# State-space mixer: the order of GpSimd's products and sums, and the depth of two buffers

## The chip, the cores and the metric

One core of a Trainium2 chip runs the whole program. The time is the device time of one launch in microseconds (us). Three runs of the kernel before gave 2972.24, 2974.73 and 2974.77 us, with a median of 2974.73 us.

## The reference

Three layers on one sequence of 256 tokens of width 2048, in fp32: differential attention and an MLP; a state-space (S5) mixer with a gated projection (GLU) and an MLP; a hybrid layer of forgetting attention and a delta-rule recurrence. The change touches only the S5 mixer, whose core is this:

```python
def s5_mixer(h, a_re, a_im, log_dt, b_re, b_im, c_re, c_im, d_skip, w_glu):
    ...
    u = h.astype(F32).reshape(B, S, S5_GROUPS, S5_GROUP)      # 128 groups of 16 channels, state 64

    def per_sequence(u_s):
        bu_re = jnp.einsum('sgc,gpc->sgp', u_s, bb_re)
        bu_im = jnp.einsum('sgc,gpc->sgp', u_s, bb_im)
        _, _, x_re, x_im = lax.associative_scan(
            _scan_combine, (a_seq_re, a_seq_im, bu_re, bu_im), axis=0)
        return jnp.einsum('sgp,gcp->sgc', x_re, cr) - jnp.einsum('sgp,gcp->sgc', x_im, ci)

    y = lax.map(per_sequence, u).reshape(B, S, D)
    y = y + d_skip.astype(F32) * h.astype(F32)
    g = jax.nn.gelu(y).astype(h.dtype)
    val, gate = jnp.split(g @ w_glu, 2, axis=-1)
    return val * jax.nn.sigmoid(gate)
```

The complex recurrence x[s] = a x[s-1] + bu[s] is solved by turning it: the inputs are multiplied by the phases of a (a cosine and a sine table), a real scan with the magnitude of a runs over the turned values, and the scanned states are turned back with the same tables.

## The kernel before, in words

Nearly all of the program is a stream of fp32 matrix products on TensorE. Weights are loaded from HBM in units, split by ScalarE (`wH`, L1785) and VectorE (`wL`, L2498) into a high and a low part, and multiplied (L987, L988, L994). Between the first MLP and the GLU product lies the S5 stage. It takes the 128 groups in 16 blocks, numbered 0 to 15, of 8 groups; the 256 tokens are folded by 4 (`S5_L`), so that a scan runs over 64 positions (`S5_N`).

The order is written out by hand. Each engine has its own loop over k = 0 to 20, and `s5_steps()` (from L204) lists the same order once more to number the semaphore values. The steps of a block b, with the names used below:

- **p(b)**, ScalarE, L2135: the tokens of the block, scaled, into `up`. **u(b)**, TensorE, L1282: four transposes into one PSUM bank. **t(b)**, ScalarE, L2143: that bank copied into `ut`, "the turned inputs". t(b) waits for u(b) and, from b = 4, for y(b-4), which read the place that is overwritten.
- **d(b)**, ScalarE, L2151: the decay table `dd` of the block.
- **g(b)**, TensorE, L1296: the products of `ut` with the input matrices `gt` into the bank `wk[b % 2]`; it waits for t(b) and for the scan z(b-2), which read that bank.
- **rotate and combine**, VectorE, L3014 and L3022: the phases applied, into `rc[b % 3]` and the bank.
- **z(b)**, VectorE, L3031: two scans, into `rc`. **n(b)**, ScalarE, L2158: a negated copy of one half.
- **zc(b)**, GpSimd, L899: the scanned states times the cosine table; it waits for z(b). **zs(b)**, L901: times the sine table; it waits for n(b). **x(b)**, L905: the sum of the two, into `xs[b % 2]`; it waits for its own zs(b) and, from b = 2, for y(b-2).
- **y(b)**, TensorE, L1311 to L1313: 24 products, of `ut`, of `xs` and of the output matrices; it waits for x(b). **e(b)**, ScalarE, L2171: two GELUs of the result.
- once in two blocks, for the pair j: **h(j)**, TensorE, L1326: eight transposes, after e(2j+1); **H(j)**, ScalarE, L2189: the high part `hH`; **hL(j)**, VectorE, L3046: the low part.

What stands in a row in step k of the loop: on TensorE u(k), g(k-1), y(k-4), and with k even and at least 6 also h((k-6)/2), in steps 16 to 19 then a unit of the GLU product (`first_unit`, L1341 to L1348). On ScalarE p(k+1), t(k), d(k), n(k-2), e(k-4), and H. On VectorE z(k-2), rotate and combine of k-1, and hL. So hL(j) stands after z(2j+4) and before z(2j+5). SyncE loads `gt`, `rt` (the phase tables) and `ft` of later blocks as the slots come free (from L579): the `rt` of block k+1 waits for zs(k-3).

`U2`, from which p reads, is filled by 32 DMAs that GpSimd issues just ahead of its first product (L890); they read `xn`, which lies at the start of the area `mix`.

Of the kernel before, what the change touches and what calls it, by code (L numbers as in the profile page):

```python
# [17 lines left out]
ALU = mybir.AluOpType  # L18
# [185 lines left out]
def s5_steps():  # L204
# [12 lines left out]
    for b in range(S5_B):  # L217
        pool += [("zc", b), ("zs", b), ("x", b)]
    return pe, act, dve, pool
# [19 lines left out]
def build(nc, I, out):  # L239
    with ExitStack() as ctx:  # L240
# [83 lines left out]
        ft = at("xt", 14, "ft", [P, 3, 4, 2, S5_L * S5_C])  # L324
        ut = at("xt", 20, "ut", [P, 4, 4, S5_N])
        up = at("xt", 24, "up", [P, 2, 2 * P])
        dd = at("xt", 26, "dd", [P, 3, 4, S5_N])
        rc = [at("gain", 0, "rc0", [P, 2, 2, 4, S5_N]), at("gain", 4, "rc1", [P, 2, 2, 4, S5_N]),
              at("mix", 0, "rc2", [P, 2, 2, 4, S5_N])]
        hd = at("mix", 4, "hd", [P, 2, S5_L, P])  # L330
        zz = at("stg", 0, "zz", [P, 2, 2, 4, S5_N])
        xs = at("stg", 4, "xs", [P, 2, 2, 4, S5_N])
# [341 lines left out]
        def _(pool):  # L674
# [217 lines left out]
            def s5_states():  # L892

                for b in range(S5_B):
                    w, n = rc[b % 3], b % 2
                    blocks = w[:].rearrange("p a r x n -> p (a r) x n")
                    table = lambda c: rt[:, b % 4, :, c].unsqueeze(1).broadcast_to([P, 2, 4, S5_N])
                    pool.wait_ge(s_dve, SDVE["z", b, 1])
                    SPOOL.mark(s_pool, nc.gpsimd.tensor_tensor(zz[:, 0], blocks[:, 2:4], table(0), ALU.mult), "zc", b)  # L899
                    pool.wait_ge(s_act, SACT["n", b])  # L900
                    SPOOL.mark(s_pool, nc.gpsimd.tensor_tensor(zz[:, 1], blocks[:, 1:3], table(1), ALU.mult), "zs", b)  # L901
                    if b >= 2:
                        pool.wait_ge(s_pe, SPE["y", b - 2])
                    pool.wait_ge(s_pool, SPOOL["zs", b])
                    SPOOL.mark(s_pool, nc.gpsimd.tensor_tensor(xs[:, n, :, :, 1:], zz[:, 0, :, :, 0:S5_N - 1], zz[:, 1, :, :, 0:S5_N - 1],  # L905
                                                               ALU.add), "x", b)
                    pool.wait_ge(s_pool, SPOOL["x", b])

# [59 lines left out]
        def _(pe):  # L968
# [317 lines left out]
            def states_of(b):  # L1286
# [6 lines left out]
                for x in range(4):  # L1293
                    for r in range(2):
                        for g in range(2):
                            last = nc.tensor.matmul(bank[quad[g], (4 * r + x) * S5_N:(4 * r + x + 1) * S5_N],  # L1296
                                                    gt[quad[g], b % 3, x, r], ut[quad[g], b % 4, x], start=True, stop=True)
                SPE.mark(s_pe, last, "g", b)

            def outputs_of(b):  # L1300
# [5 lines left out]
                for e in range(2):  # L1306
                    for h in range(2):
                        x = 2 * h + e
                        for g in range(2):
                            o = acc[0][g][quad[h], e * 64:(e + 1) * 64]  # L1310
                            nc.tensor.matmul(o, ut[quad[g], b % 4, x], Tt[quad[g], S5_HP * h + 2 * b + e], start=True, stop=False)  # L1311
                            nc.tensor.matmul(o, xs[quad[g], b % 2, 0, x], ft[quad[g], b % 3, x, 0], start=False, stop=False)
                            last = nc.tensor.matmul(o, xs[quad[g], b % 2, 1, x], ft[quad[g], b % 3, x, 1], start=False, stop=True)  # L1313
# [459 lines left out]
        def _(act):  # L1773
# [365 lines left out]
            def turned_inputs(b):  # L2139
                act.wait_ge(s_pe, SPE["u", b])  # L2140
                if b >= 4:
                    act.wait_ge(s_pe, SPE["y", b - 4])
                SACT.mark(s_act, nc.scalar.copy(ut[:, b % 4].rearrange("p x n -> p (x n)"), acc[1][0][:, 0:4 * S5_N]), "t", b)  # L2143

# [1413 lines left out]
```

## Time and profile before

| | us |
|---|---|
| median of three runs | 2974.73 |
| the profiled execution, its own time | 2972.28 |
| its span, first to last instruction | 2970.6 |
| TensorE busy | 2925.4 |
| VectorE busy | 1779.9 |
| ScalarE busy | 1396.5 |
| GpSimd busy | 369.1 |

The span leaves out what lies ahead of the first instruction and behind the last one: 2972.28 - 2970.6 = 1.7 us. Busy time is a sum over the whole program; the S5 stage lies at about 1135 to 1230 us from the span's start, and only there is GpSimd busy without a pause for long. A timeline merges a run of equal instructions that follow one another into one row with a count; an instruction can start while the one ahead of it on its engine is still draining, so what one costs its engine is the distance from start to start. A row ends with the idle time ahead of it and what ended that idle time.

### The profile page before, as it was taken

The numbers are of one execution on the slowest core, as the hardware profiler recorded it, in microseconds if no ns is written. First come the engines' busy times: TensorE is split into PE (matmuls) and PEld (weight loads), VectorE is DVE, ScalarE is ACT, GpSimd is POOL, SyncE is SP. The second block draws the span as 40 slices with busy tenths as digits, with TensorE's granted clock in tenths as the row PEclk, the third lists the DMA queues.
The fourth block names the chain that finished last, engine by engine and source line by source line (L and its number), as shares of the span: only waits on it lengthen the run. The fifth ranks groups of instructions, "written<-read, shape, count | busy, mean of one in ns | idle before, by whom it ended". The sixth has DMA issues, their size and how long they took to land.

```text
span 2970.6 us, 45464 instructions
## 1 busy us (share of the span) xinstructions
PE 2925.4 (98%) x17635; PEld 2440.1 (82%) x17635; DVE 1779.9 (60%) x2032; ACT 1396.5 (47%) x1947; POOL 369.1 (12%) x424
## 2 busy tenths in 40 slices
PE   9999999999999998999999999999999999998898
PEld 8888788888888887888888888888888888887787
DVE  5555657755766667555555555555644666665765
ACT  5555544343443447444434444344544444663344
POOL 2000010890000676200000000000000001000000
PEclk9999999999999999999999999999999999999999
DMA  7555476776666887566666566665666678661364
GB/s 251 174 171 170 156 211 202 239 230 198 191 210 219 235 257 225 162 191 215 185 191 190 188 190 187 194 185 187 191 180 189 200 203 242 219 202 50 119 212 166
DMA packets 301236, 577.56 MB, mean 194 GB/s; under 512 B 21465, under 2 KB 40153, under 8 KB 299378
## 3 DMA queue, kind: packets, MB, share of 16 engines
q1 hardware_dynamic: 284832, 522.06, 56.9%
q0 software_dynamic: 10992, 43.07, 5.0%
q10 hardware_dynamic: 5218, 9.67, 1.0%
q8 instruction: 142, 2.33, 0.3%
q14 instruction: 52, 0.43, 0.0%
HBM read 546.96 MB, written 21.50 MB: 191 GB/s over the span
## 4 chain that ended last, share of the span: by engine, by line
PE 95%; DVE 2%; ACT 1%; DMA 1%; issue 1%; ACTq 0%; POOL 0%; SPq 0%; DVEq 0%; POOLq 0%
PE acc L987 28%; PE acc L994 28%; PE acc L988 28%; PE tp L1002 2%; PE acc L1727 1%; PE acc L1720 1%; PE acc L1721 1%; PE wk L1296 1%; DMA raw<-in_mlp_w_dram 1%; PE acc L1311 0%; PE acc L1619 0%; PE wk L1629 0%; PE tp L1629 0%; PE wk L1130 0%; PE tp L1151 0%
## 5 line engine op out<-in xcount | busy, mean ns | idle before, releaser
L2498 DVE TENSOR_TENSOR wL<-raw,wH 128x1024 fp32r<-128x1024 f32 (+1 forms) x968 | 1204.4, 1253 | 1078.6 <-ACT wH L1785 1076.8
L1785 ACT CAST wH<-raw 128x1024 fp32r<-128x1024 f32 (+1 forms) x968 | 1008.6, 1046 | 1349.0 <-PE acc L994 1174.6
L987 PE MATMUL acc<-wH,xH 128*128 128x512 f32 (+1 forms) x2208 | 864.6, 392 | 0.3
L988 PE MATMUL acc<-wH,xL 128*128 128x512 f32 (+1 forms) x2208 | 855.0, 388 | 0.0
L994 PE MATMUL acc<-wL,xH 128*128 128x512 f32 (+1 forms) x2208 | 587.0, 388 | 0.1
L987 PE MATMUL acc<-wH,hH 128*128 128x512 f32 x1472 | 575.6, 391 | 1.9 <-DVE hL L2559 1.9
L988 PE MATMUL acc<-wH,hL 128*128 128x512 f32 x1472 | 572.9, 389 | 0.0
L987 PEld LDWEIGHTS acc<-wH,xH 128*128 128x128 f32 x2208 | 414.8, 188 | 84.6 <-issue 1.0
L994 PEld LDWEIGHTS acc<-wL,xH 128*128 128x128 f32 x2208 | 412.6, 188 | 85.9 <-DVE wL L2498 0.5
L988 PEld LDWEIGHTS acc<-wH,xL 128*128 128x128 f32 x2208 | 414.9, 188 | 82.5 <-issue 0.5
L994 PE MATMUL acc<-wL,hH 128*128 128x512 f32 x1472 | 393.5, 389 | 0.0
L987 PEld LDWEIGHTS acc<-wH,hH 128*128 128x128 f32 x1472 | 276.4, 188 | 58.9 <-DVE hL L2559 2.4
L994 PEld LDWEIGHTS acc<-wL,hH 128*128 128x128 f32 x1472 | 276.3, 188 | 57.4
L988 PEld LDWEIGHTS acc<-wH,hL 128*128 128x128 f32 x1472 | 276.4, 188 | 56.6
L915 POOL DMA_DIRECT2D prev<-stgs x8 | 4.3, 538 | 1081.5 <-ACT stgs L2293 1081.5
L2559 DVE TENSOR_TENSOR hL<-tp,hH 128x512 fp32r<-128x512 f32 x80 | 51.3, 683 | 7.6 <-ACT hH L1843 7.5
L1720 PE MATMUL acc<-wH,xH 128*128 128x512 f32 x128 | 50.4, 394 | 1.2 <-DVE xL L2559 1.0
L1721 PE MATMUL acc<-wH,xL 128*128 128x512 f32 x128 | 49.9, 390 | 0.0
L1002 PEld LDWEIGHTS tp<-ident,stgs 128*128 128x128 f32 x384 | 44.6, 140 | 6.2
L1002 PE MATMUL tp<-ident,stgs 128*128 128x128 f32 x384 | 49.6, 272 | 0.0
L760 POOL DMA_DIRECT2D sv<-in_b_a_re_dram x1 | 0.5, 545 | 385.7 <-PE tp L1002 385.7
L1843 ACT CAST hH<-tp 128x512 fp32r<-128x512 f32 x80 | 42.8, 587 | 9.5 <-PE tp L1002 9.5
(543 smaller groups left out, 2191.3 us busy)
## 6 DMA issues: line engine op xcount, KB each, us to landing
raw<-in_mlp_w_dram SPq DMA_DIRECT2D x512, 512.0 KB, 3.9
raw<-in_w_in_dram SPq DMA_DIRECT2D x192, 512.0 KB, 4.3
raw<-in_a_w_in_dram SPq DMA_DIRECT2D x96, 512.0 KB, 3.9
raw<-in_b_w_glu_dram SPq DMA_DIRECT2D x64, 512.0 KB, 3.8
raw<-in_a_w_out_dram SPq DMA_DIRECT2D x32, 512.0 KB, 3.8
raw<-in_w_out_dram SPq DMA_DIRECT2D x32, 512.0 KB, 4.3
raw<-in_w_proj_fox_dram SPq DMA_DIRECT2D x16, 512.0 KB, 5.2
raw<-in_w_proj_rwkv_dram SPq DMA_DIRECT2D x16, 512.0 KB, 4.7
```

What stands on the lines that cost most here:

```text
L987: nc.tensor.matmul(bank, aH[:, k, rows], wH[:, j % SPLIT, u, 0:n], start=k == 0, stop=False)
L988: nc.tensor.matmul(bank, aL[:, k, rows], wH[:, j % SPLIT, u, 0:n], start=False, stop=False)
L994: last = nc.tensor.matmul(bank, aH[:, k, rows], wL[:, j % SPLIT, u, 0:n], start=False, stop=k == KT - 1)
L1002: last = nc.tensor.transpose(dst, src, ident[:])
L1296: last = nc.tensor.matmul(bank[quad[g], (4 * r + x) * S5_N:(4 * r + x + 1) * S5_N], gt[quad[g], b % 3, x, r], ut[quad[g], b % 4, x], start ...
L1720: nc.tensor.matmul(bank, xH[:, k, rows], wH[:, j % SPLIT, u], start=k % 8 == 0, stop=False)
L1721: nc.tensor.matmul(bank, xL[:, k, rows], wH[:, j % SPLIT, u], start=False, stop=False)
L1727: last = nc.tensor.matmul(bank, xH[:, k, rows], wL[:, j % SPLIT, u], start=False, stop=k % 8 == 7)
L1785: nc.scalar.copy(wH[:, j % SPLIT, :, 0:n], raw[:, j % RAW, :, 0:n]).then_inc(high_done, 1)
L1843: nc.scalar.copy(dst, tp[bank][:]).then_inc(group_high, 1)
L2498: nc.vector.tensor_tensor(wL[:, j % SPLIT, :, 0:n], raw[:, j % RAW, :, 0:n], wH[:, j % SPLIT, :, 0:n].bitcast(F32), ALU.subtract).then_inc ...
L2559: nc.vector.tensor_tensor(dL, tp[bank][:], dH.bitcast(F32), ALU.subtract).then_inc(group_free, 1)
```

## The change

Three things are changed in the S5 stage; nothing is computed otherwise.

1. GpSimd's order. Before it was zc(b), zs(b), x(b) for each block. Now zc(0), zs(0) come first, and then for each block zc(b+1), x(b), zs(b+1). The instructions, their shapes and their number (48) stay. The wait at the end of each block for its own x goes; it is made once, after the last block.
2. The scratch `zz` of zc and zs has two places, for even and odd blocks: one where it was, the other 4 KiB at `mix` + 8 KiB. There lay `xn`, so zc(1) waits for all of the 32 DMAs that read it. zc(b) from b = 2 names x(b-2) among its waits.
3. `ut` has five places for four: t(b) waits for y(b-5) where it waited for y(b-4). `up` and `dd` move up by 1 KiB.

The order of the other engines' instructions stays as it was. On GpSimd, the start of the stage before. `zz` is the scratch, `rc0`, `rc1` and `rc2` are the scanned states of three blocks in turn, and `xs` is the sum:

```order
L899 TENSOR_TENSOR zz_102<-rc0_98,rt_93 128x512 [waits s_dve]
L901 TENSOR_TENSOR zz_102<-rc0_98,rt_93 128x512 [waits s_act]
L905 TENSOR_TENSOR xs_103<-zz_102 128x8x63 [waits s_pool]
L899 TENSOR_TENSOR zz_102<-rc1_99,rt_93 128x512 [waits s_dve,s_pool]
L901 TENSOR_TENSOR zz_102<-rc1_99,rt_93 128x512 [waits s_act]
L905 TENSOR_TENSOR xs_103<-zz_102 128x8x63 [waits s_pool]
L899 TENSOR_TENSOR zz_102<-rc2_100,rt_93 128x512 [waits s_dve,s_pool]
L901 TENSOR_TENSOR zz_102<-rc2_100,rt_93 128x512 [waits s_act]
L905 TENSOR_TENSOR xs_103<-zz_102 128x8x63 [waits s_pool,s_pe]
```

The same place of the changed kernel:

```order
L897 TENSOR_TENSOR zz0_102<-rc0_98,rt_93 128x512 [waits s_dve]
L897 TENSOR_TENSOR zz0_102<-rc0_98,rt_93 128x512 [waits s_act]
L897 TENSOR_TENSOR zz1_103<-rc1_99,rt_93 128x512 [waits u_in2,u_in1,u_in3,u_in0,s_dve]
L921 TENSOR_TENSOR xs_104<-zz0_102 128x8x63 [waits s_pool]
L897 TENSOR_TENSOR zz1_103<-rc1_99,rt_93 128x512 [waits s_act]
L897 TENSOR_TENSOR zz0_102<-rc2_100,rt_93 128x512 [waits s_pool,s_dve]
L921 TENSOR_TENSOR xs_104<-zz1_103 128x8x63 [waits s_pool]
L897 TENSOR_TENSOR zz0_102<-rc2_100,rt_93 128x512 [waits s_act]
```

The third row is zc(1); it now stands ahead of x(0), and it waits for VectorE's scan z(1) and for the DMAs. The end of the stage on GpSimd, before:

```order
L899 TENSOR_TENSOR zz_102<-rc2_100,rt_93 128x512 [waits s_dve,s_pool]
L901 TENSOR_TENSOR zz_102<-rc2_100,rt_93 128x512 [waits s_act]
L905 TENSOR_TENSOR xs_103<-zz_102 128x8x63 [waits s_pool,s_pe]
L899 TENSOR_TENSOR zz_102<-rc0_98,rt_93 128x512 [waits s_dve,s_pool]
L901 TENSOR_TENSOR zz_102<-rc0_98,rt_93 128x512 [waits s_act]
L905 TENSOR_TENSOR xs_103<-zz_102 128x8x63 [waits s_pool,s_pe]
```

The same place of the changed kernel:

```order
L921 TENSOR_TENSOR xs_104<-zz1_103 128x8x63 [waits s_pool,s_pe]
L897 TENSOR_TENSOR zz0_102<-rc2_100,rt_93 128x512 [waits s_act]
L897 TENSOR_TENSOR zz1_103<-rc0_98,rt_93 128x512 [waits s_pool,s_dve]
L921 TENSOR_TENSOR xs_104<-zz0_102 128x8x63 [waits s_pool,s_pe]
L897 TENSOR_TENSOR zz1_103<-rc0_98,rt_93 128x512 [waits s_act]
L921 TENSOR_TENSOR xs_104<-zz1_103 128x8x63 [waits s_pool,s_pe]
```

The sum x(14), the fourth row, stands behind the cosine product of block 15, the third row; before, it stood ahead of it. The last sum has no product ahead of it but its own.

```diff
--- before.py
+++ after.py
@@ -215,7 +215,7 @@
         if 1 <= k <= S5_B:
             dve += [("rc", k - 1), ("rs", k - 1), ("v", k - 1, 0), ("v", k - 1, 1)]
     for b in range(S5_B):
-        pool += [("zc", b), ("zs", b), ("x", b)]
+        pool += [("zc", 0), ("zs", 0)] * (b == 0) + [("zc", b + 1)] * (b + 1 < S5_B) + [("x", b)] + [("zs", b + 1)] * (b + 1 < S5_B)
     return pe, act, dve, pool
 
 
@@ -322,13 +322,13 @@
         gt = at("xt", 0, "gt", [P, 3, 4, 2, S5_P])
         rt = at("xt", 6, "rt", [P, 4, 4, 2, S5_N])
         ft = at("xt", 14, "ft", [P, 3, 4, 2, S5_L * S5_C])
-        ut = at("xt", 20, "ut", [P, 4, 4, S5_N])
-        up = at("xt", 24, "up", [P, 2, 2 * P])
-        dd = at("xt", 26, "dd", [P, 3, 4, S5_N])
+        ut = at("xt", 20, "ut", [P, 5, 4, S5_N])
+        up = at("xt", 25, "up", [P, 2, 2 * P])
+        dd = at("xt", 27, "dd", [P, 3, 4, S5_N])
         rc = [at("gain", 0, "rc0", [P, 2, 2, 4, S5_N]), at("gain", 4, "rc1", [P, 2, 2, 4, S5_N]),
               at("mix", 0, "rc2", [P, 2, 2, 4, S5_N])]
         hd = at("mix", 4, "hd", [P, 2, S5_L, P])
-        zz = at("stg", 0, "zz", [P, 2, 2, 4, S5_N])
+        zz = [at("stg", 0, "zz0", [P, 2, 2, 4, S5_N]), at("mix", 8, "zz1", [P, 2, 2, 4, S5_N])]
         xs = at("stg", 4, "xs", [P, 2, 2, 4, S5_N])
         m01 = at("low", 0, "m01", [P, S5_N])
         choose = at("low", 0.5, "choose", [P, MT, P])
@@ -891,20 +891,38 @@
 
             def s5_states():
 
+                def turned(b, c):
+                    blocks = rc[b % 3][:].rearrange("p a r x n -> p (a r) x n")
+                    table = rt[:, b % 4, :, c].unsqueeze(1).broadcast_to([P, 2, 4, S5_N])
+                    return nc.gpsimd.tensor_tensor(zz[b % 2][:, c], blocks[:, 2 - c:4 - c], table, ALU.mult)
+
+                def cosines(b):
+                    pool.wait_ge(s_dve, SDVE["z", b, 1])
+                    if b == 1:
+                        for q in range(QT):
+                            pool.wait_ge(u_in[q], 16 * S5_L * MT)
+                    if b >= 2:
+                        pool.wait_ge(s_pool, SPOOL["x", b - 2])
+                    SPOOL.mark(s_pool, turned(b, 0), "zc", b)
+
+                def sines(b):
+                    pool.wait_ge(s_act, SACT["n", b])
+                    SPOOL.mark(s_pool, turned(b, 1), "zs", b)
+
+                cosines(0)
+                sines(0)
                 for b in range(S5_B):
-                    w, n = rc[b % 3], b % 2
-                    blocks = w[:].rearrange("p a r x n -> p (a r) x n")
-                    table = lambda c: rt[:, b % 4, :, c].unsqueeze(1).broadcast_to([P, 2, 4, S5_N])
-                    pool.wait_ge(s_dve, SDVE["z", b, 1])
-                    SPOOL.mark(s_pool, nc.gpsimd.tensor_tensor(zz[:, 0], blocks[:, 2:4], table(0), ALU.mult), "zc", b)
-                    pool.wait_ge(s_act, SACT["n", b])
-                    SPOOL.mark(s_pool, nc.gpsimd.tensor_tensor(zz[:, 1], blocks[:, 1:3], table(1), ALU.mult), "zs", b)
+                    if b + 1 < S5_B:
+                        cosines(b + 1)
                     if b >= 2:
                         pool.wait_ge(s_pe, SPE["y", b - 2])
                     pool.wait_ge(s_pool, SPOOL["zs", b])
-                    SPOOL.mark(s_pool, nc.gpsimd.tensor_tensor(xs[:, n, :, :, 1:], zz[:, 0, :, :, 0:S5_N - 1], zz[:, 1, :, :, 0:S5_N - 1],
+                    z = zz[b % 2]
+                    SPOOL.mark(s_pool, nc.gpsimd.tensor_tensor(xs[:, b % 2, :, :, 1:], z[:, 0, :, :, 0:S5_N - 1], z[:, 1, :, :, 0:S5_N - 1],
                                                                ALU.add), "x", b)
-                    pool.wait_ge(s_pool, SPOOL["x", b])
+                    if b + 1 < S5_B:
+                        sines(b + 1)
+                pool.wait_ge(s_pool, SPOOL["x", S5_B - 1])
 
             def previous_tokens():
 
@@ -1294,7 +1312,7 @@
                     for r in range(2):
                         for g in range(2):
                             last = nc.tensor.matmul(bank[quad[g], (4 * r + x) * S5_N:(4 * r + x + 1) * S5_N],
-                                                    gt[quad[g], b % 3, x, r], ut[quad[g], b % 4, x], start=True, stop=True)
+                                                    gt[quad[g], b % 3, x, r], ut[quad[g], b % 5, x], start=True, stop=True)
                 SPE.mark(s_pe, last, "g", b)
 
             def outputs_of(b):
@@ -1308,7 +1326,7 @@
                         x = 2 * h + e
                         for g in range(2):
                             o = acc[0][g][quad[h], e * 64:(e + 1) * 64]
-                            nc.tensor.matmul(o, ut[quad[g], b % 4, x], Tt[quad[g], S5_HP * h + 2 * b + e], start=True, stop=False)
+                            nc.tensor.matmul(o, ut[quad[g], b % 5, x], Tt[quad[g], S5_HP * h + 2 * b + e], start=True, stop=False)
                             nc.tensor.matmul(o, xs[quad[g], b % 2, 0, x], ft[quad[g], b % 3, x, 0], start=False, stop=False)
                             last = nc.tensor.matmul(o, xs[quad[g], b % 2, 1, x], ft[quad[g], b % 3, x, 1], start=False, stop=True)
                 SPE.mark(s_pe, last, "y", b)
@@ -2138,9 +2156,9 @@
 
             def turned_inputs(b):
                 act.wait_ge(s_pe, SPE["u", b])
-                if b >= 4:
-                    act.wait_ge(s_pe, SPE["y", b - 4])
-                SACT.mark(s_act, nc.scalar.copy(ut[:, b % 4].rearrange("p x n -> p (x n)"), acc[1][0][:, 0:4 * S5_N]), "t", b)
+                if b >= 5:
+                    act.wait_ge(s_pe, SPE["y", b - 5])
+                SACT.mark(s_act, nc.scalar.copy(ut[:, b % 5].rearrange("p x n -> p (x n)"), acc[1][0][:, 0:4 * S5_N]), "t", b)
 
             def decays(b):
 
```

## Rows read from the trace of the kernel before

**Rows 1.** The page's chain of waits, shares of the span by engine
```profile
PE 95%; DVE 2%; ACT 1%; DMA 1%; issue 1%; ACTq 0%; POOL 0%; SPq 0%; DVEq 0%; POOLq 0%
```

**Rows 2.** Windows: us, busy PE, PEld, DVE, ACT, POOL (count), PEclk, DMA, GB/s
```profile
1166.23:1174.38 8.15, 7.11 (x178) 6.34 (x178) 7.42 (x14) 6.81 (x26) 7.52 (x7) 1.00 0.73 214
...
1200.00:1210.00 10.00, 9.94 (x129) 8.11 (x128) 5.35 (x7) 3.46 (x9) 8.97 (x7) 1.00 0.18 51
```

**Rows 3.** Waits, 1135 to 1215: in total, times, longest
```profile
ACT ut L2143 <- PE acc L1313: 11.3, 12, 2.9
...
DVE hL L3046 <- ACT hH L2189: 7.9, 6, 3.3
...
DVE rc L3014 <- DMA U<-xn: 0.2, 1, 0.2
...
POOL zz L899 <- DVE rc L3031: 5.0, 6, 3.1
```

**Rows 4.** ScalarE by time: start, us, engine, line, tiles
```profile
1166.23 0.37 ACT L2143 COPY ut<-acc 128x256 f32<-128x256 f32 x1 [1.17 <-PE acc L1313]
...
1168.09 1.10 ACT L2189 CAST hH<-acc 128x512 fp32r<-128x512 f32 x1
...
1174.38 0.37 ACT L2143 COPY ut<-acc 128x256 f32<-128x256 f32 x1 [1.17 <-PE acc L1313]
```

**Rows 5.** VectorE by time
```profile
1169.22 1.10 DVE L3046 TENSOR_TENSOR hL<-acc,hH 128x512 fp32r<-128x512 f32 x1 [0.56 <-ACT hH L2189]
1170.23 1.25 DVE L3031 TENSOR_TENSOR_SCAN rc<-dd,wk 128x256 f32<-128x256 f32 x2
...
1173.57 1.26 DVE L3031 TENSOR_TENSOR_SCAN rc<-dd,wk 128x256 f32<-128x256 f32 x2
```

**Rows 6.** TensorE by time
```profile
1171.63 1.15 PE L1296 MATMUL wk<-ut,gt 64*64 64x64 f32 x32 [0.22 <-ACT dd L2151]
...
1172.58 0.28 PE L1311 MATMUL acc<-Tt,ut 64*64 64x64 f32 x2
```

**Rows 7.** GpSimd by time
```profile
1171.62 1.27 POOL L899 TENSOR_TENSOR zz<-rc,rt 128x512 f32<-128x512 f32 x1 [0.27 <-DVE rc L3031]
1172.86 1.27 POOL L901 TENSOR_TENSOR zz<-rc,rt 128x512 f32<-128x512 f32 x1
1174.27 1.26 POOL L905 TENSOR_TENSOR xs<-zz 128x504 f32<-128x504 f32 x1
```

**Rows 8.** TensorE by time, last blocks of the stage
```profile
1196.08 1.15 PE L1296 MATMUL wk<-ut,gt 64*64 64x64 f32 x32 [1.53 <-ACT dd L2151]
...
1197.03 0.28 PE L1311 MATMUL acc<-Tt,ut 64*64 64x64 f32 x2
...
1198.66 0.98 PE L1326 MATMUL acc<-ident,hd 64*128 64x64 f32 x8
...
1208.83 0.98 PE L1326 MATMUL acc<-ident,hd 64*128 64x64 f32 x8
```

**Rows 9.** ScalarE by time, last blocks of the stage
```profile
1209.84 1.08 ACT L2189 CAST hH<-acc 128x512 fp32r<-128x512 f32 x1 [0.46 <-PE acc L1326]
```

**Rows 10.** GpSimd by time, first two products
```profile
1141.55 1.26 POOL L899 TENSOR_TENSOR zz<-rc,rt 128x512 f32<-128x512 f32 x1 [3.13 <-DVE rc L3031]
...
1144.00 1.27 POOL L901 TENSOR_TENSOR zz<-rc,rt 128x512 f32<-128x512 f32 x1 [1.19 <-ACT rc L2158]
```

**Rows 11.** VectorE by time: scans of blocks 3, 5 and 13
```profile
1150.88 1.26 DVE L3031 TENSOR_TENSOR_SCAN rc<-dd,wk 128x256 f32<-128x256 f32 x2
...
1162.06 1.27 DVE L3031 TENSOR_TENSOR_SCAN rc<-dd,wk 128x256 f32<-128x256 f32 x2
...
1194.66 1.27 DVE L3031 TENSOR_TENSOR_SCAN rc<-dd,wk 128x256 f32<-128x256 f32 x2
```

**Rows 12.** VectorE and GpSimd by time, after the last scan
```profile
1205.72 1.98 DVE L2498 TENSOR_TENSOR wL<-raw,wH 128x1024 fp32r<-128x1024 f32 x1 [2.31 <-ACT wH L1785]
...
1206.76 2.05 POOL L905 TENSOR_TENSOR xs<-zz 128x504 f32<-128x504 f32 x1
```

## The prediction

> **What bounds the kernel now.** I read the page's chain of waits first: 95% of the span is TensorE [rows 1]. The change touches only the S5 stage, so the rest of the program can only be moved as a whole by it. Then the windows. In two blocks of the stage, 8.15 us, TensorE is busy 7.11 us, VectorE 7.42, GpSimd 7.52 and ScalarE 6.81: no engine is full, and all four are nearly so. From 1200 us TensorE is busy 9.94 us of 10 [rows 2]. So a stage that reaches y(12), where the dense part begins, some microseconds earlier or later moves the end by as much, and what happens behind y(12) is hidden unless TensorE is made to wait there.
>
> The waits of the stage name the loop: t waits for the end of y, 11.3 us in all; hL waits for H, 7.9 us; GpSimd waits for the scan, 5.0 us, of which 3.1 us are its first wait [rows 3]. The loop by time, from start to start: t(8) at 1166.23, H(1) at 1168.09 (1.86, in which ScalarE also does d, n and e) [rows 4]; hL(1) at 1169.22 (1.13), z(7) at 1170.23 (1.01) [rows 5]; g(9) at 1171.63 (1.40), y(6) at 1172.58 (0.95) [rows 6]; t(10) at 1174.38 (1.80) [rows 4]. The sum is 8.15 us for two blocks. The page puts the wait of g(9) down to d on ScalarE; the scan ends at 1171.48, 0.15 us ahead of g, and g's semaphore is the scan's. Scans z(5) and z(13), four rounds apart, stand at 1162.06 and 1194.66 [rows 11]: 32.60 = 4 x 8.15. GpSimd is not in this loop: zc(7) starts at 1171.62 and x(7) at 1174.27, ends at 1175.53 [rows 7], and y(7), one block of some 4 us behind y(6) at 1172.58, has about 1 us to spare.
>
> **The change part by part.**
>
> *The fifth place of ut.* t(b) waits for y(b-5), which ended a block earlier. That opens the loop above between y and t. Alone it would leave VectorE as the next limit: 8.15 less the 0.56 us that hL waited [rows 5] is 7.59 us for two blocks. Behind this wait stand d, n, e and H on ScalarE; they come earlier too.
>
> *The own wait of GpSimd.* From zc to zs, where nothing is waited for, is 1.24 us from start to start; from zs to x, where its end is waited for, is 1.41 us [rows 7]. With another product between them every step should be 1.24 us, 3 x 1.24 = 3.72 a block and 7.44 for two. That is below 7.59, so GpSimd would not be full.
>
> *x(b) behind zc(b+1).* This costs. z(7) starts at 1170.23, z(8) only at 1173.57 and ends at 1174.83 [rows 5], but zs(7) ended at 1174.13 and x(7) could start at 1174.27 [rows 7]. Now zc(8) comes first: it starts no earlier than 0.14 us behind the scan's end, at 1174.97, and x(7) at 1176.21 on the old times, 1.9 us late, more than the 1 us to spare. In the other parity it is worse, since z(b+1) is the scan that stands behind hL. So y(b) waits for x(b), x(b) for z(b+1), and with b even h stands right behind y(b) on TensorE, H behind h, hL behind H, z(b+3) behind hL. That is a new loop over two blocks, from start to start:
>
> - z to zc 1.40 (1170.23 to 1171.62 is 1.39, 1194.66 to 1196.08 for another waiter is 1.42) [rows 5, 7, 8, 11]
> - zc to x 1.24 [rows 7]
> - x to y 1.41: 1.26 for x itself [rows 7] and 0.15 for the signal. No row shows TensorE waiting for GpSimd. By the nearest rows it is 0.15 (scan to g) [rows 5, 6], at least 0.03 (H's end to hL) [rows 4, 5], and I allow up to 0.5, since GpSimd's ends are rough; I take 0.15.
> - y to h 1.63 (1197.03 to 1198.66) [rows 8]
> - h to H 1.01 (1208.83 to 1209.84) [rows 8, 9]
> - H to hL 1.13, hL to z 1.01 [rows 4, 5]
>
> The sum is 8.83 us for two blocks, 0.68 more than 8.15. g(b+3), which stands ahead of y(b), needs z(b+1) too but is through 1.40 + 0.95 = 2.35 us behind its start, where x(b) makes y(b) wait until 4.05; so x is last.
>
> *The start.* zc(0) and zs(0) stay at 1141.55 and 1144.00 [rows 10]. Then GpSimd runs without a break, 1.24 apart: zc(1) 1145.24, x(0) 1146.48, zs(1) 1147.72, zc(2) 1148.96, x(1) 1150.20, zs(2) 1151.44, zc(3) 1152.68 (z(3) has ended by 1150.88 + 1.26 = 1152.14 [rows 11]), x(2) 1153.92. y(2) follows 1.41 later at 1155.33, h(0) at 1156.96, H(0) 1157.97, hL(0) 1159.10, z(5) at 1160.11. Before it stood at 1162.06 [rows 11]: 1.95 us gained, because ScalarE no longer sits in front of t. Here zc(1) has the new wait for the 32 DMAs; VectorE's wait for the same ones lasted 0.2 us and ended about 1145.0 [rows 3], 0.25 us before zc(1) is due. I take nothing for it; as much as 1.5 us if they land later.
>
> *The end.* Four rounds from z(5): z(13) at 1160.11 + 4 x 8.83 = 1195.43. y(12) behind it by 1.40 + 1.24 + 1.41 = 4.05, at 1199.48. Before it stood at 1197.03 [rows 8]. The stage comes to its dense part 2.45 us later. In three terms: 1.95 gained at the start, 4 x 0.68 = 2.72 lost in the rounds, 4.05 - 2.37 = 1.68 lost from z(13) at 1194.66 to y(12) at 1197.03; the sum is 2.45. Behind y(12) TensorE has a GLU unit of over 2.5 us ahead of each y, and x(13) to x(15), some 4 us apart, keep up; their slack is about 1 us at x(14), which now waits for z(15).
>
> At the end of the stage a VectorE split took 1.98 us where its mean on the page is 1.25, and the sum x(15) beside it 2.05 where others took 1.26 [rows 7, 12]. The Trainium skill (SBUF — State Buffer, "SBUF: two separate sides") says that a VectorE instruction with both inputs in SBUF and a GpSimd one that reads SBUF take turns for a whole instruction; by that rule, with which these two rows agree, the split of unit 4, moved against GpSimd's order, could catch x(14) and not x(15), and eat its slack: the sum would be up to 0.3 us more. In the loop itself each VectorE instruction has an input in PSUM, and the rule asks for nothing there.
>
> The loads: `rt` of block k+1 waits for zs(k-3) as before, and zs keeps its distance from z; SyncE's queue is not held.
>
> The sum is made on the profiled execution: 2972.28 + 2.45 = 2974.73. The median of the runs shown lies 2.45 us above that execution, so for a median I forecast 2974.73 + 2.45 = 2977.2 us.
>
> **The rivals.**
>
> *A. The loop through x does not close, and VectorE's 7.59 us decide.* For it: every share of work is below 7.6, and both edits remove a wait. Against: the order on GpSimd puts z(b+1) ahead of x(b) in plain words. Time: 1.95 at the start and 4 x 0.56 = 2.24 in the rounds, 4.2 us faster, 2970.5.
>
> *B. Gains and losses cancel.* If a signal from GpSimd takes as little as 0.03 us and h does not need all of y, a round is 8.6 and the sum 1.95 gained, 1.8 and 1.3 lost: +1.2. With a shorter wait at the start this is 2974.7 to 2976.
>
> *C. Longer rounds.* If GpSimd keeps 1.41 where I took 1.24, and the signal takes 0.5, a round is 9.35: 4 x 1.20 = 4.80, and 2.20 at the end, and of the start 1.4 is left: +5.6, 2980.3. With late DMAs 1.5 more.
>
> *D. TensorE's clock falls.* In a round TensorE would be idle 8.83 - 7.11 = 1.72 us, mostly in one piece ahead of y, where before it was 1.04 in two. From the point at which such a pause halves the granted clock, the work of a round at the 1.2 GHz level would be up to 7.11 us more: at least one round pays it, 2977.2 + 7.1 = 2984.3. Against: g(15) started behind 1.53 us of idle time [rows 8], and the granted clock of the stretch behind it, from 1200 us, is 1.00 [rows 2]. The Trainium skill (TensorE: Matmul & The Clock Gate, "Part 1: The HAM clock gate") says that an idle stretch sends the array back to half its clock; by that rule longer pauses are a risk, and this trace shows none at the length that is near.
>
> **How the numbers follow.** What this measurement can tell from no change is about 0.2%, 5.9 us: faster is below 2968.8, slower above 2980.7. The forecast, its own range 2975.5 to 2979.5, has 0.66; A 0.10, B 0.10, C 0.10, D 0.04. Faster by over 0.2% needs a gain beyond all of A: 0.02. Slower: D and the upper third of C, 0.07. Within 0.2%: 0.91. The runs shown spread by 2.5 us, which widens either side; the range 2972.5 to 2981.0 leaves out most of A and all of D.
>
> **What would show it.** In the changed kernel's trace TensorE waits in the stage for GpSimd's x (no such row before), and t no longer waits for y. Scans z(7) to z(13) stand 8.83 us apart for two blocks, z(5) at about 1160.1, y(12) at 1199.5, zc to x 1.24. GpSimd's wait for the scan grows from 5.0 us to about 5 x 1.4 + 3.1 = 10. It is wrong if y(12) stands before 1197.0, if rounds are of 8.15 or less, or if a window of the stage has a granted clock below 1.

## The result, and the profile after

| | median, us | runs | lowest to highest |
|---|---|---|---|
| before | 2973.64 | 22 | 2970.48 to 2976.16 |
| changed | 2977.30 | 22 | 2972.84 to 2981.74 |

The ratio is 1.0014, with a 95% interval of 1.0009 to 1.0020: the changed kernel is slower by 2.7 to 5.9 us. That is clear of no change; the median step, 3.7 us, is below the 5.9 us (0.2%) that the prediction took as the limit of "slower", and the upper end of the interval touches it. The forecast was 2977.2 us and 2.45 us slower. The median sits on the forecast, but the kernel before has come out at 2973.64 in the longer row of runs, so the step that was measured is 3.7 us and not 2.45.

The profiled execution took 2975.47 us with a span of 2973.8, which is 3.2 us above that of before. The waits of the stage in the changed kernel, from 1135 to 1215 us (engine and line, what for, total, times, longest):

```profile
PE acc L1329 <- issue: 6.7, 5, 1.4
...
PE wk L1314 <- DVE rc L3049: 0.5, 1, 0.5
...
ACT hd L2189 <- PE acc L1331: 11.8, 10, 3.3
...
DVE hL L3064 <- ACT hH L2207: 11.5, 7, 3.3
...
POOL zz L897 <- DVE rc L3049: 12.4, 7, 3.1
```

t's wait for y, 11.3 us before [rows 3], is gone: it has no row. hL's wait for H went from 7.9 to 11.5 us and GpSimd's for the scan from 5.0 to 12.4 (about 10 were forecast; the rest is a wait of 2.5 us for the last scan, at 1205 us). TensorE's first row is the new wait: y (L1329 is its first line) stood still 5 times, 6.7 us in all. The profile writes "issue", its word for waiting for nothing that it can see. GpSimd's rows show what it was. This is one round by time, TensorE's rows first:

```profile
1180.64 0.30 PE L1329 MATMUL acc<-Tt,ut 64*64 64x64 f32 x2 [1.32 <-issue]
...
1182.30 0.79 PE L1344 MATMUL acc<-ident,hd 64*128 64x64 f32 x5
```

```profile
1183.32 1.09 ACT L2207 CAST hH<-acc 128x512 fp32r<-128x512 f32 x1 [0.46 <-PE acc L1344]
```

```profile
1176.71 1.26 DVE L3049 TENSOR_TENSOR_SCAN rc<-dd,wk 128x256 f32<-128x256 f32 x2
...
1184.44 1.11 DVE L3064 TENSOR_TENSOR hL<-acc,hH 128x512 fp32r<-128x512 f32 x1 [1.13 <-ACT hH L2207]
1185.45 1.25 DVE L3049 TENSOR_TENSOR_SCAN rc<-dd,wk 128x256 f32<-128x256 f32 x2
```

```profile
1178.05 1.28 POOL L897 TENSOR_TENSOR zz<-rc,rt 128x512 f32<-128x512 f32 x1 [1.47 <-DVE rc L3049]
1179.28 1.26 POOL L921 TENSOR_TENSOR xs<-zz 128x504 f32<-128x504 f32 x1
```

z(9) starts at 1176.71, zc(9) at 1178.05 after 1.47 us of waiting, x(8) at 1179.28, y(8) at 1180.64, that is 0.10 us behind x's end; h(3) at 1182.30, H(3) at 1183.32, hL(3) at 1184.44, z(11) at 1185.45. From start to start 1.34, 1.23, 1.36, 1.66, 1.02, 1.12 and 1.01: 8.74 us. This is the loop of the prediction, link by link. It sits in the trace as follows, with the first of the 30 products on constants taken as the start of the stage, here

```profile
1128.33 3.51 PE L1272 MATMUL acc<-ones 128*128 128x128 f32 x30
```

and in the kernel before

```profile
1129.24 3.51 PE L1254 MATMUL acc<-ones 128*128 128x128 f32 x30
```

| | before | changed | forecast | measured |
|---|---|---|---|---|
| z(5) from the stage's start | 32.82 | 30.73 | -1.95 | -2.09 |
| z(5) to z(13), four rounds | 32.60 | 35.14 | +2.72 | +2.54 |
| z(13) to y(12) | 2.37 | 3.91 | +1.68 | +1.54 |
| y(12) to y(13) | 5.49 | 8.37 | 0 | +2.88 |

The rows for it, in the changed kernel:

```profile
1159.06 1.27 DVE L3049 TENSOR_TENSOR_SCAN rc<-dd,wk 128x256 f32<-128x256 f32 x2
...
1194.20 1.25 DVE L3049 TENSOR_TENSOR_SCAN rc<-dd,wk 128x256 f32<-128x256 f32 x2
```

```profile
1198.11 0.30 PE L1329 MATMUL acc<-Tt,ut 64*64 64x64 f32 x2 [1.37 <-issue]
```

```profile
1200.44 1.44 PE L1344 MATMUL acc<-ident,hd 64*128 64x64 f32 x8
1201.80 0.79 PE L1359 MATMUL tp<-wH,hH 128*128 128x512 f32 x1
```

```profile
1206.48 0.33 PE L1329 MATMUL acc<-Tt,ut 64*64 64x64 f32 x2
```

and y(13) in the kernel before:

```profile
1202.52 0.32 PE L1311 MATMUL acc<-Tt,ut 64*64 64x64 f32 x2
```

The first three lines of the table add up to +2.0 us, where 2.45 was forecast. The fourth was not in the sum. Between y(12) and y(13) TensorE does the rest of y(12), h(5) and the first GLU unit, the same work in both kernels. h(5) took 0.98 us before [rows 8] and takes 1.44 here, and from y(12) to h(5) it is 2.33 us where it was 1.63. The windows show why (columns as in [rows 2]; the third number from the end is the granted clock):

```profile
1196.00:1198.00 2.00, 0.74 (x26) 0.61 (x21) 1.86 (x5) 0.23 (x2) 2.00 (x3) 1.00 0.47 139
1198.00:1200.00 2.00, 1.89 (x46) 1.92 (x47) 1.99 (x4) 0.42 (x1) 2.00 (x3) 0.68 0.00 0
1200.00:1202.00 2.00, 1.94 (x17) 1.52 (x14) 0.76 (x2) 0.54 (x3) 2.00 (x3) 0.50 0.14 32
1202.00:1204.00 2.00, 2.00 (x5) 1.61 (x6) 0.94 (x1) 1.02 (x1) 0.93 (x1) 0.50 0.29 99
1204.00:1206.00 2.00, 2.00 (x7) 1.53 (x7) 1.32 (x3) 0.42 (x1) 0.60 (x1) 0.61 0.00 0
1206.00:1208.00 2.00, 2.00 (x50) 1.64 (x49) 0.00 (x0) 0.00 (x0) 2.00 (x3) 1.00 0.00 0
```

The granted clock fell to 0.50, the 1.2 GHz level, for some 6.8 us. By the shares of the windows it fell at about 1198.7 us, 0.6 us into y(12), and came back at about 1205.5. Ahead of the fall TensorE had stood still for 0.54 us (g(15), behind z(13)) and then for 1.37 us (y(12), behind x(12)).

### The profile page after: what moved, and what is told of

It reads as the page before. It is cut to its first block, busy times and chain, and to the rows that moved or that the text cites. A ratio compares the mean times of both kernels' runs of the same rounds, so it can differ in the third digit from the quotient of the medians.

```text
span 2973.8 us, 45464 instructions
## 1 busy us (share of the span) xinstructions
PE 2927.4 (98%) x17635; PEld 2441.9 (82%) x17635; DVE 1776.6 (60%) x2032; ACT 1397.2 (47%) x1947; POOL 367.3 (12%) x424
## 3 DMA queue, kind: packets, MB, share of 16 engines
q8 instruction: 142, 2.33, 0.3%
## 4 chain that ended last, share of the span: by engine, by line
PE 95%; DVE 2%; DMA 1%; issue 1%; ACT 1%; SPq 0%; ACTq 0%; DVEq 0%
PE acc L1005 28%; PE acc L1012 27%; PE acc L1006 27%; PE tp L1020 2%; PE acc L1745 1%; PE acc L1738 1%; PE acc L1739 1%; DMA raw<-in_mlp_w_dram 1%; PE wk L1314 1%; PE acc L1637 0%; PE acc L1329 0%; PE wk L1647 0%; PE tp L1647 0%; PE tp L1359 0%; PE wk L1148 0%
```

## The experiments

In all of them "before" ran on the same chip beside the kernels compared: median 2972.80 us in the first group of runs, 2973.26 in the second, 2973.61 in the third. A round is the distance of two odd scans. All the numbers by one table first:

| kernel | median, us | ratio to before, 95% interval | rounds z(5) to z(13), us |
|---|---|---|---|
| changed | 2977.30 | 1.0014 (1.0009 to 1.0020) | 8.77 8.88 8.74 8.75 |
| changed, again | 2976.50 | 1.0014 (1.0005 to 1.0022) | 8.74 8.76 8.74 8.74 |
| five places alone | 2969.41 | 0.9988 (0.9979 to 0.9997) | 7.53 7.51 7.50 7.67 |
| order and two scratches alone | 2983.51 | 1.0036 (1.0024 to 1.0048) | 10.62 12.00 9.73 9.70 |
| old order, rest new | 2969.56 | 0.9988 (0.9979 to 0.9997) | 7.60 7.74 7.74 7.74 |
| changed, turn ahead of y | 2967.41 | 0.9980 (0.9971 to 0.9989) | 8.19 7.51 7.49 7.66 |
| before, turn ahead of y | 2993.19 | 1.0066 (1.0048 to 1.0083) | 13.48 13.60 13.61 13.62 |
| old order, rest new, turn ahead | 2968.82 | 0.9984 (0.9975 to 0.9993) | 8.76 7.54 7.50 7.51 |
| changed, TensorE kept busy ahead of y | 2973.39 | 1.0000 (0.9991 to 1.0009) | 8.74 8.73 8.72 8.73 |
| the same, and ahead of g(3) | 2974.30 | 1.0007 (0.9998 to 1.0016) | 8.71 8.73 8.73 8.75 |
| changed, turn ahead, busy ahead of g(3) | 2968.06 | 0.9986 (0.9977 to 0.9995) | 8.19 7.50 7.50 7.69 |
| old order, rest new, turn ahead, busy ahead of g(3) | 2967.90 | 0.9981 (0.9972 to 0.9990) | 8.67 7.51 7.52 7.51 |

### The two halves of the change apart

The fifth place of `ut` in the kernel before, nothing else (and `up`, `dd` moved up by 1 KiB):

```diff
-        ut = at("xt", 20, "ut", [P, 4, 4, S5_N])
+        ut = at("xt", 20, "ut", [P, 5, 4, S5_N])
...
-                if b >= 4:
-                    act.wait_ge(s_pe, SPE["y", b - 4])
+                if b >= 5:
+                    act.wait_ge(s_pe, SPE["y", b - 5])
```

> The kernel before with only the fifth place of ut (t waits for y(b-5)); GpSimd's order and its one scratch as before. Theory (the loss of the change sits in x(b) behind zc(b+1); the fifth place is a gain by itself): t no longer waits for y, VectorE becomes the limit, rounds of two blocks from z(5) to z(13) of 7.6 to 7.9 us where before had 8.15 and the change 8.79; z(5) about 2 us earlier in the stage; the program 2 to 4 us faster than before, ratio near 0.999. Rival (the fifth place, with t, d and the transposes issued earlier, is what crowds the other engines): rounds of 8.15 or longer, the program not faster than before.

Measured: 3.4 us under the before beside it, scans in rounds of 7.5 us. The 7.59 that the prediction took for VectorE's limit was 0.1 too long. The rival falls.

VectorE is not the only limit here, though. GpSimd stands still nowhere between 1168 and 1200 us:

```profile
1177.79 1.26 POOL L905 TENSOR_TENSOR xs<-zz 128x504 f32<-128x504 f32 x1
1179.12 1.28 POOL L899 TENSOR_TENSOR zz<-rc,rt 128x512 f32<-128x512 f32 x1
1180.35 1.28 POOL L901 TENSOR_TENSOR zz<-rc,rt 128x512 f32<-128x512 f32 x1
1181.77 1.26 POOL L905 TENSOR_TENSOR xs<-zz 128x504 f32<-128x504 f32 x1
```

From x(8) to x(9) it is 3.98 us: 1.33 and 1.42 where GpSimd waits for its own instruction, 1.23 where it does not. So the y's fall behind the scans. y(8), y(10) and y(12) stand at 1179.14, 1187.13 and 1195.10, 7.98 us apart, and the last one had to wait 0.58 us:

```profile
1195.10 0.29 PE L1311 MATMUL acc<-Tt,ut 64*64 64x64 f32 x2 [0.58 <-issue]
```

From the stage's start to y(12) the profiled execution takes 66.3 us, 1.5 less than before.

The other half, the changed kernel with four places:

```diff
-        ut = at("xt", 20, "ut", [P, 5, 4, S5_N])
+        ut = at("xt", 20, "ut", [P, 4, 4, S5_N])
...
-                if b >= 5:
-                    act.wait_ge(s_pe, SPE["y", b - 5])
+                if b >= 4:
+                    act.wait_ge(s_pe, SPE["y", b - 4])
```

> The changed kernel with ut back in four places: GpSimd's new order and the two scratches alone. Theory: x(b) is late by the wait for z(b+1), and now t(b+4) waits for y(b) as well, so both chains run in one: rounds from z(5) to z(13) of about 9.9 us, y(12) some 8 us later in the stage than before, the program 8 to 12 us slower than before (ratio 1.003 to 1.004; with a longer stretch at the 1.2 GHz level more). Rival (the order is harmless, the stage is limited elsewhere): within 2 us of before, rounds of 8.2 us.

Measured: 10.7 us over before. Two rounds are 9.7 us, as expected; the two longer ones lie in a stretch at half the clock, in the profiled execution from 1168 to 1182 us; a second one begins just ahead of y(12), at 1210.60 us:

```profile
1168.00:1182.00 14.00, 12.65 (x199) 11.62 (x201) 9.48 (x17) 6.70 (x25) 10.48 (x10) 0.53 0.43 131
1208.00:1218.00 10.00, 8.49 (x96) 7.32 (x97) 7.20 (x13) 2.66 (x7) 7.39 (x6) 0.58 0.15 48
```

So the harm is in GpSimd's order and scratch, the gain in the fifth place. Which of the two, order or scratch, was the next question. The changed kernel with the old order, and the two scratches, the five places and the missing own wait kept:

```diff
-                cosines(0)
-                sines(0)
                 for b in range(S5_B):
-                    if b + 1 < S5_B:
-                        cosines(b + 1)
+                    cosines(b)
+                    sines(b)
...
-                    if b + 1 < S5_B:
-                        sines(b + 1)
```

> The changed kernel with GpSimd's old order zc(b), zs(b), x(b); the two scratches, the fifth place of ut and the missing own wait at the end of a block stay. With the fifth place alone the rounds measured 7.5 us and GpSimd's own wait was still there. Theory (the order is the only harmful part; the second scratch and the missing own wait are worth nothing, because VectorE and not GpSimd limits a round): rounds of 7.5 us, the time of the kernel with the fifth place alone within 1 us, so about 3.5 us faster than before (ratio near 0.9988). Rival (the second scratch or its wait for the DMAs costs by itself): 1.5 us or more slower than the fifth place alone.

Measured: 2969.56 us, 0.15 us from the fifth place alone; the rounds were 0.1 to 0.2 us longer than expected, the time was not. What costs is the order alone. The rounds of 7.74 are GpSimd's own:

```profile
1178.13 1.26 POOL L919 TENSOR_TENSOR xs<-zz 128x504 f32<-128x504 f32 x1
1179.35 2.50 POOL L897 TENSOR_TENSOR zz<-rc,rt 128x512 f32<-128x512 f32 x2
1181.99 1.26 POOL L919 TENSOR_TENSOR xs<-zz 128x504 f32<-128x504 f32 x1
```

It has no pause between 1168 and 1200 us here either, and needs 3.86 us a block (3.98 with the own wait at the end of a block). In the profiled executions y(12) comes 65.3 us behind the stage's start, 1.0 us sooner than with the fifth place alone, although the clock was at 0.50 for 3.4 us at the stage's start. So the missing own wait is worth about a tenth of a microsecond a block; the medians, with intervals of some 5 us in width, can't tell that from nothing. The second scratch by itself was not measured.

### Taking y out of the loop

If x(b) late behind z(b+1) matters only because h stands behind y(b), then h and H moved ahead of y and e must take away the loss. h(j) needs e(2j+1), of the block before, and nothing of y(2j+2):

```diff
-                if 4 <= k < S5_B + 4:
-                    outputs_of(k - 4)
                 if k >= 6 and k % 2 == 0:
                     mixed_turn((k - 6) // 2)
+                if 4 <= k < S5_B + 4:
+                    outputs_of(k - 4)
```

and likewise H ahead of e in ScalarE's loop.

> The changed kernel with h(j) ahead of y(2j+2) on TensorE and H(j) ahead of e(2j+2) on ScalarE; h(j) needs only e of the block before, so nothing else is moved. Theory: this takes y out of the loop z, zc, x, y, h, H, hL, z. y and x are as late as before behind the scan, but nobody waits for them; rounds from z(5) to z(13) fall from 8.79 to about 7.6 us, VectorE being the limit, hL waits hardly any more, y(12) about 7 us earlier in the stage than in the changed kernel, the program 6 to 9 us faster than the changed kernel and 3 to 5 us faster than before (ratio about 0.9985). Rival (the rounds are longer because GpSimd or VectorE hinder each other, or because of the waits for the scan as such): rounds stay at 8.5 us or more. A second rival, that only the TensorE clock costs: rounds stay at 8.79 and the time falls by at most 3 us.

Measured: 2967.41 us, 5.4 under the before beside it and 9 to 10 under the changed kernel. VectorE in a round:

```profile
1170.16:1177.67 7.51, 7.33 (x180) 6.52 (x177) 7.34 (x15) 6.83 (x26) 6.73 (x7) 1.00 0.71 210
1177.67:1185.16 7.49, 7.32 (x178) 6.50 (x176) 7.32 (x14) 6.72 (x26) 7.42 (x8) 1.00 0.70 211
```

```profile
1176.00 0.76 DVE L3040 TENSOR_TENSOR wk<-rc,wk 128x256 f32<-128x256 f32 x2
1176.67 1.10 DVE L3064 TENSOR_TENSOR hL<-acc,hH 128x512 fp32r<-128x512 f32 x1
1177.67 1.26 DVE L3049 TENSOR_TENSOR_SCAN rc<-dd,wk 128x256 f32<-128x256 f32 x2
...
1181.01 1.26 DVE L3049 TENSOR_TENSOR_SCAN rc<-dd,wk 128x256 f32<-128x256 f32 x2
```

VectorE (third of the busy times) is at 7.32 of 7.49 us, and hL at 1176.67 waits for nothing. TensorE (the first) is as full, 7.32 us. GpSimd's order is that of the changed kernel, with the wait for z(b+1) ahead of x(b) in it. The total of its waits is half of what it was, since the scans come sooner:

```profile
POOL zz L897 <- DVE rc L3049: 6.3, 5, 3.1
```

and TensorE has no row for y among its waits. Both rivals fall: GpSimd and VectorE beside each other do not hinder the loop, and the order as such costs nothing where nobody stands behind y.

The same move in the kernel before:

> The kernel before with h(j) ahead of y(2j+2) and H(j) ahead of e(2j+2), and nothing else. With four places t(b) waits for y(b-4), which now stands behind h, and e and y of a block wait for H. Theory: the loop of before through t, H, hL, z, g and y gets h into it, and y(b+1) waits for an e that stands behind H: rounds of 8.5 to 9.5 us, the program 2 to 7 us slower than before. So the turn ahead helps only where t does not wait for y(b-4). Rival (h ahead of y helps by itself, whatever the places): rounds under 8.15 us and the program faster than before.

Measured: 2993.19 us, 19.9 slower; the sign was as expected, the size was not. In its profile the clock fell at about 1163 us and stayed at 0.50 for the rest of the loop:

```profile
1190.61:1204.22 13.61, 12.22 (x181) 10.87 (x180) 7.51 (x14) 6.73 (x26) 7.60 (x7) 0.50 0.40 122
```

A round is 13.61 us, and TensorE is busy 12.22 us of it, where the same work takes 7.11 at full clock [rows 2]. By these busy times, 5.1 us more in each of four rounds, the clock made most of the loss. The fastest of its six runs, 2981.96 us at a mean granted clock of 0.998, is the nearest to what the expected rounds alone would cost; the others had 0.988 to 0.993. What a round at full clock would be was not measured.

### The clock's share

The changed kernel ran a second time, beside the others.

> The changed kernel again, beside the others on one chip. Theory: as measured, 3 to 5 us slower than before (ratio 1.001 to 1.002), rounds of 8.79 us, with a mean granted clock lower in the slower executions; the same kernel with TensorE kept busy ahead of y was level with before, so the clock accounts for about half of the loss. Rival (the first measurement was off by the chip): level with before, or more than 5 us slower.

Measured: ratio 1.0014 again. Its profiled execution has the fall of the clock at the same place, from about 1199.1 to 1206.0 us, and y(12) to y(13) is 1207.19 - 1198.87 = 8.32 us. So the fall in y(12) came in both profiled executions of this kernel. By the clock of each run, rounded to three digits: the six runs at 0.998 average 2975.5 us, the three at 0.997 2978.7.

Then four products on constants in TensorE's pause ahead of y(b), b = 4, 6, 8, 10 and 12; y's wait for x now stands behind its wait for e and behind these products:

```diff
-                pe.wait_ge(s_pool, SPOOL["x", b])
                 if b:
                     pe.wait_ge(s_act, SACT["e", b - 1, 1])
+                if 4 <= b <= 12 and b % 2 == 0:
+                    awake(4)
+                pe.wait_ge(s_pool, SPOOL["x", b])
```

> The changed kernel with four 128x128 products on constants (about 1.05 us, results unused) ahead of y(b) for b = 4, 6, 8, 10 and 12, in the pause in which TensorE waits for x(b). In the profile of the changed kernel the granted clock fell to 0.50 from about 1198.7 to 1205.2 us, behind y(12); that stretch cost 2.8 us. Theory (the pauses ahead of y bring the clock down): granted clock 1.00 in the whole stage, rounds as in the changed kernel (8.79), the program 1 to 3 us faster than the changed kernel, so 1 to 2.5 us slower than before. Rival (the fall has nothing to do with these pauses, or the profiled execution is not typical): the same time as the changed kernel within 1 us, and a fall of the clock somewhere.

Measured: 2973.39 us, level with before, 3.1 us under the changed kernel of the next group by the medians, 3.9 under the first. Rounds stay at 8.73. In its profile the clock is at 1.00 from 1140 us to the end of the stage, and has fallen early, at 1136 to 1140 us, ahead of the loop: "1.00 in the whole stage" was wrong. So these were added too:

```diff
+                if k == 4:
+                    awake(4)
                 if 4 <= k <= S5_B:
                     states_of(k - 1)
```

> The changed kernel with four products on constants (about 1.05 us) ahead of y(b) for b = 4, 6, 8, 10, 12, and four more ahead of g(3), where TensorE waits for a DMA. The rounds should stay at 8.74 to 8.79 us. Theory (the loss of the changed kernel has two parts, the longer rounds and a stretch at half the clock behind y(12)): granted clock 1.00 at 1190 to 1210 us, and the program 0 to 2 us slower than before, 2 to 4 us faster than the changed kernel. Rival (the products only pushed the fall elsewhere): as slow as the changed kernel.

Measured: 2974.30 us. The profile has no window of the stage under 1.00:

```profile
1190.00:1200.00 10.00, 8.88 (x188) 7.91 (x188) 8.61 (x16) 5.48 (x19) 8.69 (x9) 1.00 0.47 148
1200.00:1210.00 10.00, 9.93 (x128) 8.23 (x128) 6.17 (x10) 3.75 (x8) 8.66 (x7) 1.00 0.10 28
```

and what is left of the pause ahead of y is now put down by name to GpSimd's x:

```profile
PE acc L1331 <- POOL xs L921: 1.0, 5, 0.2
```

This execution separates the two shares of the loss. Its y(12) and y(13) are

```profile
1200.01 0.33 PE L1331 MATMUL acc<-Tt,ut 64*64 64x64 f32 x2 [0.23 <-POOL xs L921]
...
1205.57 0.33 PE L1331 MATMUL acc<-Tt,ut 64*64 64x64 f32 x2
```

that is 5.56 us apart at the full clock, where the changed kernel took 8.37 with the same order. From the stage's start, at 1130.20, to y(13) it is 75.4 us, against 73.3 before and 78.2 in the changed kernel: 2.1 us for the rounds and 2.8 for the clock.

Against before this is +0.7 us by the medians and +2.1 by the ratio, with an interval from -0.6 to +4.8 us. The rounds' share of 2.0 us lies in it; so does nothing. The clock's share is the difference to the changed kernel, 2 to 4 us by medians of different groups, against 2.8 in the profiles.

### The fastest version

GpSimd's old order with everything else, and the turn ahead; then the same with four products ahead of g(3), and those in the new order too:

> GpSimd's old order, two scratches, five places of ut, and the turn h, H ahead of y, e. Theory: VectorE limits the rounds at 7.5 us here as with either GpSimd order, since y and x are out of the loop; z(5) some 1.3 us earlier than without the turn ahead; time within 1 us of the 2967.4 us of the new order with the turn ahead, and 0.5 to 2 us under the old order without it (2969.6). Rival (GpSimd's own wait makes the old order slower once VectorE is the limit): 1 us or more above 2967.4.

> The last one with four products on constants ahead of g(3). Theory: as with the new order, where the same four products measured 2968.1 against 2967.4 us, no change of more than 1 us, and no granted clock under 1.00 from 1148 us on. Rival (the clock's fall behind the wait for the DMA costs a microsecond in the mean): 1 us or more faster.

> The changed kernel with the turn h(j) and H(j) ahead, and besides four 128x128 products on constants (about 1.05 us, results unused) on TensorE ahead of g(3), where it waits for a DMA. In the profile of the kernel with the turn ahead the granted clock was at 0.50 from 1150 to about 1156 us, behind that wait. Theory: the pause there brings the clock down in a part of the executions; with the products in it the clock stays at 1.00 from 1148 us on, and the median is 0.5 to 2 us below the 2967.4 us of the turn ahead, so the fastest so far. Rival (the fall there is chance or cost nothing): the same median within 0.5 us, or 1 us more for the added products.

Measured: 2968.82, 2967.90 (ratio 0.9981, 0.9972 to 0.9990) and 2968.06 us (0.9986, 0.9977 to 0.9995). With 2967.41 for the new order without them, all four intervals overlap: with y out of the loop the order on GpSimd makes no difference that these runs can tell, and neither do the products ahead of g(3) in the median. The old order came out 1.4 us above 2967.4, outside the 1 us of its theory, but in the other group of runs, with a before that was 0.8 us higher. The gain of 0.5 to 2 us that was expected of the products ahead of g(3) in the new order did not come, though the clock stayed at 1.00 through the stage. Under the old order the products narrowed the spread, from 2964.7 to 2973.2 without them to 2965.7 to 2968.9 with them; under the new order they did not. All four beat the kernel before by 0.1 to 0.2% and the changed one by 0.3%.

## Why the prediction was right

The sign and the loop behind it were right. The median fell on the forecast in part by luck, and one thing by which the prediction said that it would be wrong did happen: a window of the stage with a granted clock below 1.

- **What bounds the kernel.** Right: only the S5 stage changed, and the loop from t through H, hL, z, g and y was its limit; with t's wait for y relaxed alone, the scans' rounds fell to 7.5 us.
- **The fifth place of ut.** Right in kind, and nearly in size for the scans: "7.59 us" was 7.50. But "alone it would leave VectorE as the next limit" left out GpSimd, which with its own waits needs 3.98 us a block. With the fifth place alone it had no pause left, and y came in rounds of 7.98.
- **GpSimd's own wait.** From zc to x it is 1.23 us in the changed kernel, 1.24 said, and three steps are 3.68, 3.72 said. In the changed kernel GpSimd waited 1.3 us for the scan in each round and was no limit of its own. Under the old order it took GpSimd from 3.98 to 3.86 us a block, which the medians don't show.
- **x(b) behind zc(b+1).** This was the step that carried the sign. A round of 8.83 was forecast and 8.785 measured; the signal from GpSimd to TensorE, taken as 0.15 from other engines' rows, is 0.10. Moving h ahead of y, with GpSimd's order as it was, took the loss away; putting the old order back did too. Both show it, from two sides.
- **The start and the end.** -1.95 and +1.68 forecast, -2.09 and +1.54 measured. The new wait for the 32 DMAs cost nothing at zc(1) in the profiled execution, where GpSimd ran without a break; with the turn ahead it was 0.6 us in one.
- **The tail behind y(12).** "What happens behind y(12) is hidden" was right for the work and wrong for the clock. Rival D, which had a chance of 0.04, did occur, at a smaller price than it was given: 2.9 us in place of 7.1. The prediction held against it that g(15) had 1.53 us of idle time at full clock. In the changed kernel two pauses, 0.54 and 1.37 us, follow in short distance at the end of the loop, where u(16) no longer fills in. With the second one filled there was no fall; that it takes both was not tested. The term for the clock is the one that was missing. The sum of the measured terms is 2.0 + 2.9 = 4.9 us, while the spans differ by 3.2: this execution was 0.9 us ahead from 200 us on, and it makes up another 0.8 between 2690 and 2850 us, where the two kernels do the same work. What differed there stays open.
- **The number.** 2977.2 against 2977.3 is better than the working deserves: the step was 3.7 us where 2.45 was said, and the before of the three runs shown stood 1.1 us above the median of 22. The working lacked the clock's 2.9 us, and the median shows only part of them.

Left open: why the clock falls in y(12) and not in an earlier round, each of which has a pause of 1.3 us (with the order alone it fell at y(4) and y(12) and not at y(8) or y(10), all behind a pause of 1.37); and what the fastest kernels lose to falls that come in some executions only. Nor do the medians follow the profiled stages: from the stage's start to y(13) the changed kernel took 4.9 us more than before, where its median is 3.7 higher, and the fifth place alone 1.5 us less, where its median is 3.4 lower. Every other kernel, too, came out lower against before by its median than by its stage. The one profiled execution of before may have been a fast one for the stage; no second one was taken.

## What to carry to other kernels

A product placed between a product and its sum hides the wait for the engine's own instruction (here 0.17 us, 1.41 to 1.24 from start to start), but it puts the sum behind whatever that product waits for; ask of every instruction moved forward whose wait the ones behind it inherit. Look next at what stands in a row behind the late one on the other engines: here the cure was not on GpSimd but in exchanging two independent steps on TensorE. And where a change adds pauses to TensorE, the sum needs a term for its clock even if every single pause was harmless before.

## What the runs showed of the hardware

- The same small fp32 products of a round took 7.11 us of TensorE at the 2.4 GHz level [rows 2] and 12.22 us at the 1.2 GHz level (before, turn ahead), 1.7 times as long. Falls of the granted clock came in the stage in seven of the twelve kernels profiled, and at different places: in the changed kernel with the turn ahead at 1150 to 1156 us, behind a wait of 1.28 us for the DMA of g(3), and it was back within the loop; in the kernel before with the turn ahead it stayed down for 65 us. That kernel lost 19.9 us in the median where 2 to 7 were expected of its waits.
- Where nothing else holds it, GpSimd took 1.23 us from start to start for such a product or sum, and 1.33 to 1.42 us where the instruction waits for the end of the one ahead of it on GpSimd. From the end of x to the start of a y that waits for it was 0.10 us.
- The long split and the long sum at the end of the stage [rows 12] have their counterpart in the changed kernel, where only the split is long:

```profile
1209.68 1.98 DVE L2516 TENSOR_TENSOR wL<-raw,wH 128x1024 fp32r<-128x1024 f32 x1 [4.36 <-ACT wH L1803]
```

```profile
1209.30 1.28 POOL L921 TENSOR_TENSOR xs<-zz 128x504 f32<-128x504 f32 x1
```

Here the split starts within x(15), which goes at full speed and ends at 1210.58; the split ends at 1211.66, 1.08 us behind. Before, the split started within zs(15) (1205.32 to 1206.61) and ended at 1207.70, 1.09 us behind it, and x(15), which started within the split, ended at 1208.81, 1.11 us behind that. By these rows each waited for the one that had started first. The Trainium skill (SBUF — State Buffer, "SBUF: two separate sides") says the same: of a GpSimd instruction and a VectorE one with two inputs in SBUF, the first to start holds the shared ports until it ends. It cost nothing at either place: y(15) came later than both, and TensorE had no pause there.
